# Scan of a two-block transformer kernel: every product as 64x64 tiles, two elementwise steps moved to GpSimd

## What is computed

```
w_log = -softplus(-(decay_w0[d] + tanh(hw) @ decay_w2[d])) - 0.5
a     = sigmoid(iclr_a0[d] + ha @ iclr_a2[d])
decay = exp(-exp(heads(w_log)))
k_d   = heads(k * (1 + (a - 1) * k_a))
...
sa = einsum('bhvk,bhk->bhv', S, -kk_t)
S  = S * w_t + sa * b_t + v_t * k_t
y  = einsum('bhvk,bhk->bhv', S, r_t)
...
bonus = sum(r * (k_d0 + k_d1) * r_k) * v
```

## Time and profile before

| | us |
|---|---|
| median of three runs | 4389.38 |
| lowest and highest | 4387.12, 4395.81 |
| profiled execution, its own time | 4392.67 |
| its span | 4390.9 |
| TensorE busy in the span | 3919.1 (89%) |
| VectorE, ScalarE, GpSimd busy | 2663.4 (61%), 1722.4 (39%), 381.3 (9%) |
| mean granted TensorE clock | 0.942 |

### The profile page before, as it was taken

The page is one execution under the profiler, slowest core; times in us unless marked ns, Lnnn a source line. Parts: engine busy times, 40 slices in busy tenths (PEclk is TensorE's granted clock), DMA queues, the critical chain, the costliest instruction groups (busy, mean ns, idle before and its releaser), DMA issues. The chain is left out here.

```text
span 4390.9 us, 79510 instructions
## 1 busy us (share of the span) xinstructions
PE 3919.1 (89%) x33222; PEld 3243.3 (74%) x33222; DVE 2663.4 (61%) x4533; ACT 1722.4 (39%) x3046; POOL 381.3 (9%) x459
## 2 busy tenths in 40 slices
PE   8998888988999998799578999979999597999997
PEld 6887656877786776587466877778888476888886
DVE  3346658875775655888455014668778644565656
ACT  3037526763564542577446112223222122222222
POOL 0000101210000000121000000033333000000002
PEclk9999988998999999899789999989999798999998
DMA  3111349982000024999310211000000230111110
GB/s 116 39 57 46 107 190 362 395 317 89 15 2 1 1 83 154 362 395 347 130 21 24 93 48 54 21 10 4 3 4 4 103 134 29 58 39 58 39 53 39
DMA packets 174673, 444.09 MB, mean 101 GB/s; under 512 B 29572, under 2 KB 83724, under 8 KB 149740
## 3 DMA queue, kind: packets, MB, share of 16 engines
q1 hardware_dynamic: 165100, 405.44, 24.5%
q0 software_dynamic: 9216, 33.56, 3.0%
HBM read 385.36 MB, written 53.49 MB: 100 GB/s over the span
## 5 line engine op out<-in xcount | busy, mean ns | idle before, releaser
L583 PE MATMUL psum<-weight_parts,h_parts 128*128 128x512 f32 (+2 forms) x2880 | 601.5, 371 | 23.5 <-DVE h_parts L784 14.8
L583 PEld LDWEIGHTS psum<-weight_parts,h_parts 128*128 128x128 f32 x2880 | 508.0, 191 | 110.9 <-DVE h_parts L784 16.6
L1906 DVE TENSOR_TENSOR weight_parts<-weights_raw,weight_parts 128x2048 fp32r<-128x2048 f32 x192 | 432.0, 2288 | 68.5 <-ACT weight_parts L1875 67.2
L1875 ACT ACTIVATE weight_parts<-weights_raw 128x2048 fp32r<-128x2048 f32 x192 | 360.6, 1919 | 100.0 <-DMA weights_raw<-in_moe_w_up 43.8
L1812 PE MATMUL psum<-weight_parts,picked_parts 128*128 128x512 f32 x1536 | 362.0, 395 | 9.2 <-DVE picked_parts L1893 9.2
L2385 PE MATMUL psum<-h_parts,up_parts 128*128 128x512 f32 x1536 | 355.2, 392 | 11.0 <-DVE up_parts L2466 11.0
L2401 PE MATMUL psum<-down_parts,hidden_parts 128*128 128x512 f32 x1536 | 353.5, 391 | 6.7 <-DVE down_parts L2471 6.7
L2385 PEld LDWEIGHTS psum<-h_parts,up_parts 128*128 128x128 f32 x1536 | 291.2, 190 | 72.7 <-DVE up_parts L2466 11.8
L1812 PEld LDWEIGHTS psum<-weight_parts,picked_parts 128*128 128x128 f32 x1536 | 288.9, 190 | 72.4 <-DVE picked_parts L1893 12.4
L2401 PEld LDWEIGHTS psum<-down_parts,hidden_parts 128*128 128x128 f32 x1536 | 290.1, 189 | 67.6 <-DVE down_parts L2471 7.1
L769 DVE TENSOR_TENSOR weight_parts<-weights_raw,weight_parts 128x512 fp32r<-128x512 f32 (+4 forms) x78 | 102.7, 1349 | 379.0 <-ACT weight_parts L652 378.9
(11 more groups left out here) (474 smaller groups left out, 7140.2 us busy)
## 6 DMA issues: line engine op xcount, KB each, us to landing
weights_raw<-in_moe_w_gate SPq DMA_DIRECT2D x64, 1024.0 KB, 13.7
weights_raw<-in_moe_w_up SPq DMA_DIRECT2D x64, 1024.0 KB, 14.2
weights_raw<-in_moe_w_down SPq DMA_DIRECT2D x64, 1024.0 KB, 12.8
w_ada<-in_w_ada SPq DMA_DIRECT2D x12, 2048.0 KB, 8.9
up_raw<-in_w_mlp_up SPq DMA_DIRECT2D x16, 1024.0 KB, 7.4
down_raw<-in_w_mlp_down SPq DMA_DIRECT2D x16, 1024.0 KB, 5.2
weights_raw<-in_even_w_in SPq DMA_DIRECT2D x10, 1024.0 KB, 5.1
weights_raw<-in_w_in SPq DMA_DIRECT2D x10, 1024.0 KB, 5.5
```

What stands on the lines that cost most here:

```text
L583: last = pe.matmul(ps[:, t, 0:width(n)], cols[:, i, KP * h + k, t * P:(t + 1) * P], part[:, n % 2, j, k, 0:width(n)], start=(h == 0 and m ...
L1875: act.activation(part[:, n % PART_SLOTS, 0], raw[:, n % RAW_SLOTS], ACT.Copy).then_inc(high, 1)
L1906: dve.tensor_tensor(part[:, n % PART_SLOTS, 1], raw[:, n % RAW_SLOTS], part[:, n % PART_SLOTS, 0].bitcast(F32), ALU.subtract).then_inc(low, 1)
```

## The change

- The lora's weights get 128 partitions: `decay_w2` on 0 to 31, `iclr_a2` on 64 to 95, the rows between set to zero by two memsets of VectorE, for which the lora's loads wait. The projection's group 12 becomes 128 columns: `hw`, then `ha` and its copies at 32, 64 and 96; for this there are two more weight loads in `rwkv`, and six more loads of convolution weights in `Condition`. Each lora product takes 64 rows and 64 columns; there are 8 for a tile instead of 4, over 128 tokens as before.
- The transposes of the two key products become 16 products of 64x64 blocks with the identity. They lie in columns 256 to 511 of two PSUM banks, and L k v moves into columns 0 to 255 of the same two banks, one half of the partitions in each.
- ScalarE's copies of turn 6 are now three: half of L k v, `b_and_k_rows`, the other half. All come after both waits. TensorE's first level waits for the first two, its second turn for the third.
- The bonus becomes 8 products of 64x64 with one column each, and is moved ahead of the output's first products, one turn earlier.
- Receptance times exponential (L3127) leaves VectorE for turn 3 of GpSimd; TensorE waits for it (`r_scaled`) ahead of the pairs. The inverse's first block (L3141, L3143) leaves VectorE for turn 6 of GpSimd.

```diff
@@ -2148,7 +2148,7 @@
...
 
-    LOADS = 18
+    LOADS = 24
...
@@ -2169,6 +2169,9 @@
...
             sp.dma_start(self.vb[14 * tap + 12:14 * tap + 13, 0:64], cw[1536:1600].unsqueeze(0)).then_inc(loaded, 16)
+            for row in (64, 96):
+                sp.dma_start(self.vb[14 * tap + 12:14 * tap + 13, row:row + 32], cw[1568:1600].unsqueeze(0))\
+                  .then_inc(loaded, 16)
...
@@ -2539,7 +2542,7 @@
...
     NT = T_ALL // P
-    widths = [P] * 12 + [64, 96]
+    widths = [P] * 13 + [96]
...
@@ -2577,8 +2580,13 @@
...
                 if p >= 2:
-                    sp.dma_start(raw_of(p)[:, :, 0:widths[j]], w_rows[:, :, starts[j]:starts[j] + widths[j]])\
+                    own = 64 if j == 12 else widths[j]
+                    sp.dma_start(raw_of(p)[:, :, 0:own], w_rows[:, :, starts[j]:starts[j] + own])\
                       .then_inc(loaded[p % 2], 16)
+                if j == 12:
+                    for row in (64, 96):
+                        sp.dma_start(raw_of(p)[:, :, row:row + 32], w_rows[:, :, starts[j] + 32:starts[j] + 64])\
+                          .then_inc(loaded[p % 2], 16)
...
@@ -2634,7 +2642,7 @@
...
                 if p >= 2:
-                    act.wait_ge(loaded[p % 2], 16 * (p // 2))
+                    act.wait_ge(loaded[p % 2], 16 * (p // 2 + (2 if order[p] == 12 else 0)))
...
@@ -2720,7 +2728,7 @@
...
     eye = c.at("chunk_identity", 55, [P, 64])
-    w2 = c.at("lora_weights", 111.5, [64, 2, 512])
+    w2 = c.at("lora_weights", 111.5, [P, 2, 512])
...
@@ -2728,7 +2736,7 @@
...
         masks.append(k)
-    loads = [(w2[32 * i:32 * i + 32, d], dram[name][0, d]) for d in (0, 1)
+    loads = [(w2[64 * i:64 * i + 32, d], dram[name][0, d]) for d in (0, 1)
...
@@ -2860,18 +2868,19 @@
...
     names = ("lora_done", "tanh_done", "log_ready", "running_ready", "exps_ready", "key_scaled", "key_ready", "scaled",
-             "ends_scaled", "pairs_done", "pairs_masked", "bk_turned", "bk_copied", "lkv_done", "lkv_copied",
+             "ends_scaled", "r_scaled", "near_ready", "pairs_done", "pairs_masked", "bk_turned", "bk_copied", "lkv_done", "lkv_copied",
...
     both = [f"{n}_{i}" for i in range(4) for n in names]
-    with stage(nc, "dve_step", "lora_loaded", "tables_loaded", *both) as (
-            block, dve_step, lora_loaded, tables_loaded, *sems):
+    with stage(nc, "dve_step", "lora_cleared", "lora_loaded", "tables_loaded", *both) as (
+            block, dve_step, lora_cleared, lora_loaded, tables_loaded, *sems):
...
         def _(sp):
+            sp.wait_ge(lora_cleared, 2)
...
@@ -2891,14 +2900,16 @@
...
                         j = 2 * g + jj
-                        for kind in (0, 1):
-                            rows = slice(32 * kind, 32 * kind + 32)
-                            last = pe.matmul(ps[:, A + kind, jj * P:(jj + 1) * P], w2[rows, d, j * P:(j + 1) * P],
-                                             rw[rows, 12, tok(t)], start=True, stop=True)
+                        for cc, C in CH:
+                            for kind in (0, 1):
+                                rows, ch = half_of(kind), j * P + 64 * cc
+                                last = pe.matmul(ps[C, A + kind, jj * P:(jj + 1) * P], w2[rows, d, ch:ch + 64],
+                                                 rw[rows, 12, tok(t)], start=True, stop=True)
...
 
+                    pe.wait_ge(s["r_scaled"], i + 1)
...
@@ -2915,18 +2926,23 @@
...
                         for jj in (0, 1):
-                            col = n * 256 + jj * P
-                            last = pe.transpose(ps[:, A, col:col + P], src[:, jj], c.ident[:])
+                            col = 256 + n * P + jj * 64
+                            for cc, C in CH:
+                                for par in (0, 1):
+                                    R = half_of(par)
+                                    last = pe.matmul(ps[C, A + par, col:col + 64], src[R, jj, C], c.ident[R, R],
+                                                     start=True, stop=True)
...
                         for cc, C in CH:
-                            last = pe.matmul(ps[C, B, slot(par, jj) * 64:(slot(par, jj) + 1) * 64],
+                            last = pe.matmul(ps[C, A + cc, slot(par, jj) * 64:(slot(par, jj) + 1) * 64],
...
                     pe.wait_ge(s["bk_copied"], i + 1)
+                    pe.wait_ge(s["lkv_copied"], 2 * i + 1)
...
@@ -2940,7 +2956,7 @@
...
                         if level == 0:
-                            pe.wait_ge(s["lkv_copied"], i + 1)
+                            pe.wait_ge(s["lkv_copied"], 2 * i + 2)
...
@@ -2975,15 +2991,21 @@
...
                             for par in (0, 1):
-                                col, h = (2 * jj + par) * 64, 4 * g + 2 * jj + par
+                                col, h = jj * 64, 4 * g + 2 * jj + par
                                 out = ps[half_of(par), A + cc, 256 + jj * 64:256 + (jj + 1) * 64]
-                                pe.matmul(out, b.tm[C, 0, col:col + 64], b.U[C, slot(par, jj)], start=True, stop=False)
-                                last = pe.matmul(out, b.tm[C, 1, col:col + 64], v_rows(C, t, slice(h * 64, h * 64 + 64)),
+                                pe.matmul(out, b.tm[C, par, col:col + 64], b.U[C, slot(par, jj)], start=True, stop=False)
+                                last = pe.matmul(out, b.tm[C, par, P + col:P + col + 64], v_rows(C, t, slice(h * 64, h * 64 + 64)),
...
                         pe.wait_ge(s["state_ready"], 2 * i + 2)
+                        for jj in (0, 1):
+                            for cc, C in CH:
+                                for par in (0, 1):
+                                    h = 4 * g + 2 * jj + par
+                                    pe.matmul(ps[C, A + par, 384 + jj:385 + jj], b.rk[half_of(par), jj, C],
+                                              rks[half_of(par), 2 * g + jj, h:h + 1], start=True, stop=True)
...
@@ -3003,11 +3025,9 @@
...
                                               start=False, stop=False)
-                                    pe.matmul(out, b.LL[C, par, 1, jj, 1, :], v_rows(C, t, slice(h * 64, h * 64 + 64)),
-                                              start=False, stop=(jj == 1))
-                        for jj in (0, 1):
-                            last = pe.matmul(ps[:, A, 384:388], b.rk[:, jj], rks[:, 2 * g + jj, 4 * g:4 * g + 4],
-                                             start=(jj == 0), stop=(jj == 1))
+                                    last = pe.matmul(out, b.LL[C, par, 1, jj, 1, :],
+                                                     v_rows(C, t, slice(h * 64, h * 64 + 64)),
+                                                     start=False, stop=(jj == 1))
...
@@ -3036,10 +3056,12 @@
...
                     act.wait_ge(s["bk_turned"], i + 1)
-                    act.activation(b.tm[:].rearrange("p a b -> p (a b)"), ps[:, A, :], ACT.Copy)\
-                       .then_inc(s["bk_copied"], 1)
                     act.wait_ge(s["lkv_done"], i + 1)
-                    act.activation(flat(b.LKV), ps[:, B, 0:256], ACT.Copy, scale=-1.0).then_inc(s["lkv_copied"], 1)
+                    act.activation(b.LKV[half_of(0)].rearrange("p h n -> p (h n)"), ps[half_of(0), A, 0:256], ACT.Copy,
+                                   scale=-1.0).then_inc(s["lkv_copied"], 1)
+                    act.activation(b.tm[:], ps[:, A:A + 2, 256:512], ACT.Copy).then_inc(s["bk_copied"], 1)
+                    act.activation(b.LKV[half_of(1)].rearrange("p h n -> p (h n)"), ps[half_of(1), B, 0:256], ACT.Copy,
+                                   scale=-1.0).then_inc(s["lkv_copied"], 1)
...
@@ -3073,13 +3095,25 @@
...
                     yield
+                    pool.wait_ge(s["exps_ready"], i + 1)
+                    pool.tensor_tensor(b.ar[:, :, 1, :], r_[:, 2 * g:2 * g + 2, tok(t)], b.e1[:], ALU.mult)\
+                        .then_inc(s["r_scaled"], 1)
...
                         .then_inc(s["ends_scaled"], 1)
-                    for _ in range(13):
+                    yield
+                    yield
+                    near = masks[d].neighbour_turned[:].unsqueeze(1).unsqueeze(1).to_broadcast([P, 2, 2, 64])
+                    pool.wait_ge(s["pairs_masked"], i + 1)
+                    pool.tensor_tensor(b.MT[:].rearrange("p (a j) n -> p a j n", a=2), b.LL[:, :, 0, :, 0, :], near,
+                                       ALU.mult).then_inc(s["near_ready"], 1)
+                    pool.wait_ge(s["near_ready"], i + 1)
+                    pool.tensor_tensor(b.MT[:], b.MT[:], eye[:].unsqueeze(1).to_broadcast([P, 4, 64]), ALU.add)\
+                        .then_inc(s["mt_ready"], 1)
+                    for _ in range(11):
...
@@ -3099,6 +3133,8 @@
...
             step = Step(dve, dve_step)
+            for row in (32, 96):
+                dve.memset(w2[row:row + 32], 0.0).then_inc(lora_cleared, 1)
...
@@ -3108,7 +3144,7 @@
...
                     emit = t >= 2
```

(12 more changed lines are left out.)

## The result

The changed kernel takes 4454.28 us (median of 4 runs, 4450.78 to 4459.28), the kernel before 4391.33 (4 runs, 4387.12 to 4395.81): a ratio of 1.0139, 95% interval 1.0126 to 1.0152. Slower, as forecast, but three times as much: +63 us where 19 were expected, and above the top of the range, 4436.

What follows compares the result with a forecast made beforehand. It took a ring of TensorE, ScalarE's tanh chain and VectorE's scan as the bound; +4 us for 40 tiles, +14 clock, +1.5 start made +19 on 4389.4, so 4408 us, range 4362 to 4436.

Steps and rivals of the forecast that it cites:

- The margin of 0.19 us: ScalarE's tanh chain ends 0.19 us before VectorE's scan starts; 0.14 us of the tanh's 0.39 us delay fits into it.
- All four signs: No ScalarE idle before the tanh, scan released by the tanh chain, longer TensorE waits before a_state, over eight low stretches.
- the collision of VectorE's product: VectorE's product beside GpSimd's new receptance product, both reading SBUF, loses 0.18 us a tile, between nothing and 0.73.
- The term of +1.5 us for the start of the scan: Two VectorE memsets delay the lora's loads before the scan's start: +1.5 us, between nothing and 3.
- the clock term: TensorE's waiting part stretches, so 16 tiles instead of 8 have a 1.2 GHz stretch, 1.7 us each: +14 us, up to +34.
- the old waits over 0.46 us more: TensorE reaches its waiting part 0.36 us earlier and leaves 0.10 later, spreading the same products over 0.46 us more.
- ScalarE's copies: Three copies ahead of the tanh take 1.06 us, at most 1.36, making the tanh 0.39 us late, at most 0.69.
- TensorE saved more than 0.36 us: Bonus -0.25, transposes +0.22 and lora -0.33 us: TensorE was to need 0.36 us less a tile, at 0.029 us an issue.
- TensorE's saving counts: Rival, chance 0.28: the tanh stays within its margin and tiles shorten by 0.6 us: 4367 us, 4350 to 4380.
- The collision and the clock together: Rival, chance 0.12: GpSimd's product always locks out VectorE's dense stretch, +0.55 us a tile: 4430 us, up to 4455.
- a low stretch in nearly each tile: Upper end of the much slower rival, chance 0.12: nearly every scan tile has time at 1.2 GHz, up to 4455 us.
- The fast case: Rival, chance 0.28, where TensorE's shorter work shortens each scan tile by 0.6 us: 4367 us, 4350 to 4380.

Runs made afterwards that it cites:

- after_filled: The changed kernel plus two unused identity products of 256 columns a tile, waiting for the tanh, ahead of TensorE's solution product: 4388.35 us.
- undo_gpsimd: The changed kernel with receptance times exponential and the inverse's first block back on VectorE: 4465.33 us.
- undo_transposes: The changed kernel with the 128-row transposes, the place of L k v and ScalarE's two copies as before: 4395.17 us.
- before_late_start: The kernel before, with both of ScalarE's copies behind the wait for L k v and no third copy: 4412.79 us.
- before_late_tanh: The kernel before, with only ScalarE's copies in the new order, three and all behind L k v: 4458.69 us.
- before_filled1: The kernel before plus one unused identity product of 256 columns a tile ahead of the solution product: 4395.38 us.
- undo_transposes_filled1: The changed kernel with transposes, L k v and ScalarE's copies as before, plus one unused 256-column product a tile ahead of the solution: 4359.95 us.
- after_dve_copy_filled1: The changed kernel with half of L k v copied by VectorE instead of ScalarE, plus one unused 256-column product a tile ahead of the solution: 4365.85 us.

## Why the prediction went wrong

**The place and the mechanism held.** The margin of 0.19 us was the number to watch: ScalarE runs without idle time into the tanh, L3048 releases the scan, TensorE waits longer ahead of the solution, there are more than eight low stretches. All four signs named ahead are there. So is the collision of VectorE's product, 0.19 us on average for 0.18 charged. But it costs nothing, as it lies ahead of the pairs, where TensorE no longer waits. The term of +1.5 us for the start of the scan is not borne out: the wait for the lora's weights did grow, by 10.71 - 9.36 = 1.35 us, but the product behind it starts at 2858.84 instead of 2859.78, since the convolution ended earlier in this trace, and the scan begins no later than before.

**The failed step is the size of the clock term:** "I expect more tiles with a low stretch, 16 instead of 8", +14 us, with up to +34. The low time went from 27.3 to 187.7 us. Against the kernel with the clock held (after_filled) that is 4454 - 4388 = 66 us. Two things in the term were too small. The number: all 27 steady tiles have a low stretch, and seven lie in the eight tiles ahead of them. The length: a stretch lasts 6.8 us, where the prediction's 1.7 us is the price of one of 3.4 to 3.6. Sixteen of those are some 55 us of low time, less than a third of what came. The price for each microsecond of low time was not too small: (415.4 - 356.6)/(187.7 - 13.7) = 0.34 us, where 1.7 for 3.6 is 0.47. The error behind it: the prediction spread the old waits over 0.46 us more, where in fact the wait ahead of the solution alone grew to over a microsecond. That the clock is the cause is shown by after_filled, with the tanh as late as before.

**Two smaller terms pushed the same way.** ScalarE's copies took 1.34 us, where 1.06 was taken and 1.36 was the upper end: the overlap of 0.1 us that successive tanh show is there behind the first copy alone (starts 0.31, 0.63 and 0.40 apart for lengths of 0.38, 0.60 and 0.38). The earlier trace rows had shown it: the two copies of before start 0.62 us apart, and the first lasts 0.60. And TensorE saved more than 0.36 us. Twelve identity products take 0.38 us, one 0.22, so they leave (0.38 - 0.22)/11 = 0.0145 us apart. The prediction had read 0.029 as what the issue allows, and it is not. The prediction named this case, but as one that helps: "TensorE's saving counts". With the tanh late it does not count, as TensorE only comes earlier to a wait whose end it does not set. This is our reading of how 0.35 us became 1.27; the two shares were not measured apart.

**The rivals.** "The collision and the clock together" (0.12) gave 4430 to 4455, which is what was measured, but only half of it was the cause: without the collision (undo_gpsimd) the kernel is no faster, while "a low stretch in nearly each tile" did come. "TensorE's saving counts" (0.28) was right in its condition: where the tanh is not held up (undo_transposes), the full-clock tile is 12.3 us, and with the clock held as well that kernel takes 4360, under the 4367 it gave.

**The fast case needs the clock.** undo_transposes has the short tile and is no faster than before, since 78.5 us of its 363.8 are low. What stays open is why: TensorE waits only up to 0.4 us ahead of the solution there (8.4 us in 26 waits over the steady scan), about as in before_late_start (8.2 in 28), which has 34.1 us of low time. Waits alone do not order these two; before_late_tanh and the changed kernel too have 21.5 and 27.6 us of waits but 85.3 and 187.7 of low time. The products of the lora as 64x64, or a shorter rest of the tile, may have a share; neither was tried alone, and the bonus showed none. That a large product in the wait brings the low time to 14 us or nothing in each of these kernels is shown; how the low time follows from what TensorE does between is not.

## What to carry to other kernels

When engines hand over in a ring, look for the margin of each chain on the engines that are *not* busy before a copy is put ahead of it: here 0.38 us on a ScalarE that was busy for 28% of the scan was worth 61 us. When TensorE's saving ends in a wait, look at the granted clock before the busy time, and price the case that every round loses it, for longer each time than before. Where such a wait can't be removed, a large product without use may fill it: here that made four kernels 27 to 66 us faster, and the kernel before, with little low time, not at all.

## What the runs showed of the hardware

64x64 products of 64 columns that rotate over all four quarters of the array leave 0.0145 us apart on average (L2933 above); those that use two, as L2939, leave (0.51 - 0.22)/10 = 0.029 apart, as L2924 did in the kernel before. The clock went to 1.2 GHz once in every tile of 15 us, for 6.8 us, although TensorE is busy for over 90% of the time and waits for 1.3 us at most. One product of 256 columns a tile, in the wait, was enough to keep it at 2.4 GHz through the 27 tiles in before_filled1, undo_transposes_filled1 and after_dve_copy_filled1; the changed kernel itself was tried with two only, and kept 13.7 us of low time. VectorE's L3155 (two inputs in SBUF) ended 0.28 us behind the end of the product of GpSimd that it met, in all 39 meetings of the changed kernel's trace: it waits for the rest of that product and not for a share of it.
